# Every projection of a two-layer decoder trunk as one plain 32-bit product in place of three split ones, with a weight ring of seven places

## The reference

```
h += rms(mixer(rms(h)));  h += rms(swiglu(rms(h)));  h += (p @ W_ple) * sigmoid(h @ W_gate)
layer 0 mixer: gated DeltaNet
  qkv,z,beta,a = x @ gdn_w_in (1024 x 6176); qkv = silu(conv4(qkv)); q,k L2-normed
  chunked delta rule, 16 heads of 128;  out = (rms(o) * silu(z)) @ gdn_w_out (2048 x 1024)
after layer 0: kv = rms(h) @ kv_w (1024 x 1536), keys and values of three attention branches
layer 1 mixer: sparse attention, 16 heads of 64; q, gates = x @ nsa_w_qg (1024 x 1072); out = o @ nsa_w_o (1024 x 1024)
swiglu, both layers: (silu(x @ W_g) * (x @ W_u)) @ ffn_w_out, hidden 2816
ple, both layers: p @ ple_w_in (256 x 1024), h @ ple_w_gate (1024 x 1024)
```

## Time and profile before

| | |
|---|---|
| median of 3 runs | 969.92 us (969.77 to 970.20) |
| the profiled execution's own time | 970.94 us |
| its span, first to last instruction | 968.9 us |
| TensorE matmul busy | 925.4 us, 96% |
| TensorE weight load busy | 781.1 us, 81% |
| VectorE busy | 583.3 us, 60% |
| ScalarE busy | 519.7 us, 54% |
| moved by DMA | 138.30 MB, mean 143 GB/s |

### The profile page before, as it was taken

How to read it: one execution, slowest core, us unless ns; L and a number is a source line. 1 busy time by engine, 2 the same in 40 slices (tenths; PEclk the granted TensorE clock), 3 DMA queues, 4 the chain that set the end, 5 groups by cost and what they waited for, 6 DMA issues and landing times.

```text
span 968.9 us, 14299 instructions
## 1 busy us (share of the span) xinstructions
PE 925.4 (96%) x5437; PEld 781.1 (81%) x5437; DVE 583.3 (60%) x965; ACT 519.7 (54%) x919; POOL 23.3 (2%) x47
## 2 busy tenths in 40 slices
PE   5999989999999999999999999998889999999998
PEld 5989978797887877888887788997567788888776
DVE  5767775666566575555544666656857555554465
ACT  6554555766766446444443548245865644444352
POOL 5000000000000000000000000000000000000000
PEclk9999999999999999999999999999999999999999
DMA  9941202021112556777655654420024566565552
GB/s 320 330 138 44 88 0 88 10 78 44 45 45 90 193 166 212 236 232 240 192 175 171 208 186 154 150 88 2 1 89 141 169 191 193 174 191 176 171 187 100
DMA packets 105755, 138.30 MB, mean 143 GB/s; under 512 B 4569, under 2 KB 76514, under 8 KB 105698
## 3 DMA queue, kind: packets, MB, share of 16 engines
q1 hardware_dynamic: 103200, 130.04, 42.0%
q0 software_dynamic: 2160, 7.36, 2.1%
q10 hardware_dynamic: 338, 0.12, 0.0%
HBM read 136.45 MB, written 1.05 MB: 142 GB/s over the span
## 4 chain that ended last, share of the span: by engine, by line
PE 79%; ACT 10%; DVE 8%; issue 2%; ACTq 0%; DMA 0%; SPq 0%; DVEq 0%
PE ps L490 16%; PE ps L492 16%; PE ps L491 16%; PE ps L469 4%; PE ps L474 4%; PE ps L476 4%; PE ps L475 4%; DVE w_lo L1561 3%; ACT w_hi L1098 3%; PE ps L705 3%; PE ps L723 3%; PE ps L938 1%; PE ps L984 1%; ACT qkvT L1495 1%; PE ps L608 1%
## 5 line engine op out<-in xcount | busy, mean ns | idle before, releaser
L1561 DVE TENSOR_TENSOR w_lo<-w_raw,w_hi 128x2048 fp32r<-128x2048 f32 (+2 forms) x100 | 220.7, 2207 | 203.4 <-ACT w_hi L1098 203.3
L1098 ACT ACTIVATE w_hi<-w_raw 128x2048 fp32r<-128x2048 f32 (+2 forms) x100 | 184.4, 1844 | 191.0 <-PE ps L492 150.0
L490 PE MATMUL ps<-w_hi,x_hi 128*128 128x512 f32 x480 | 193.0, 402 | 7.4 <-DVE gdn L1772 2.2
L492 PE MATMUL ps<-w_hi,x_lo 128*128 128x512 f32 x480 | 187.7, 391 | 0.0
L491 PE MATMUL ps<-w_lo,x_hi 128*128 128x512 f32 x480 | 187.2, 390 | 0.0
L490 PEld LDWEIGHTS ps<-w_hi,x_hi 128*128 128x128 f32 x480 | 90.2, 188 | 29.7 <-issue 7.4
L492 PEld LDWEIGHTS ps<-w_hi,x_lo 128*128 128x128 f32 x480 | 90.1, 188 | 19.4
L491 PEld LDWEIGHTS ps<-w_lo,x_hi 128*128 128x128 f32 x480 | 90.3, 188 | 16.8
L474 PE MATMUL ps<-x_hi,w_hi 128*128 128x256 f32 x320 | 92.2, 288 | 0.3 <-DVE w_lo L1607 0.3
L475 PE MATMUL ps<-x_lo,w_hi 128*128 128x256 f32 x320 | 90.9, 284 | 0.0
L490 PE MATMUL ps<-w_hi,big 128*128 128x512 f32 x224 | 89.9, 401 | 1.0 <-DVE w_lo L1561 1.0
(11 more groups left out here) (309 smaller groups left out, 1492.0 us busy)
## 6 DMA issues: line engine op xcount, KB each, us to landing
w_raw<-in_ffn_w_in SPq DMA_DIRECT2D x88, 512.0 KB, 4.5
w_raw<-in_ffn_w_out SPq DMA_DIRECT2D x40, 512.0 KB, 4.1
w_raw<-in_gdn_w_in SPq DMA_DIRECT2D x28, 512.0 KB, 4.8
gdn<-in_gdn_w_in SPq DMA_DIRECT2D x20, 512.0 KB, 8.8
w_raw<-in_gdn_w_out SPq DMA_DIRECT2D x16, 512.0 KB, 4.5
w_raw<-in_ple_w_gate SPq DMA_DIRECT2D x16, 512.0 KB, 4.5
w_raw<-in_kv_w SPq DMA_DIRECT2D x12, 512.0 KB, 4.4
qkvT<-in_cmp_w POOLq DMA_DIRECT2D x8, 512.0 KB, 5.3
```

The costliest lines, as they stand in the source:

```text
L490: mm(o, hi, w_h, start=first and kk == 0, stop=False, skip_group_check=True)
L492: return mm(o, lo, w_h, start=False, stop=end and kk == n - 1, skip_group_check=True)
L1098: A(whi[:, place(stage, q), c0:c0 + n], ring_raw(u) if stage == "qkv" else raw[:, q, 0:n], ACT.Copy).then_inc(S["hi_done"], 1)
L1561: V.tensor_tensor(wlo[:, s, c0:c0 + n], ring_raw(u) if stage == "qkv" else raw[:, q, 0:n], whi[:, s, c0:c0 + n], ALU.subtract).then_inc(S[ ...
```

## The change

All fp32r tiles go, and with them every split of weights and activations. Each product is one plain float32 matmul, read from the raw weights where they landed. The raw weights get a ring of seven places through the whole kernel. SyncE loads unit u when TensorE has done unit u-7. A unit is one transfer of its whole size, save in fin and the first two of kv, which stay two transfers (their two column groups), and unit 0. TensorE waits for the transfer itself (`arrived`). The activation items, which both engines worked on in turn, are now made by ScalarE for even numbers and by VectorE for odd ones. The hardware loops of the fin stages are written out. The first items of the compression weights (`cmp_w1`) are loaded by GpSimd every four units of fin0 in place of every two. `big` and the attention outputs lie in other storage.

The diff, cut to its core:

```diff
+TRANSFERS = [2 if n.startswith("fin") or (n == "kv" and m < 2) else 1 for n, c in STAGES for m in range(2 * c)]
-RING = 6
+RING = 7
...
-        raw = sb("w_raw", [P, 2, 8 * UW])
-        whi = sb("w_hi", [P, 2, 8 * UW], F32R)
-        wlo = sb("w_lo", [P, 2, 8 * UW], F32R)
-        xhi = sb("x_hi", [P, KD, T], F32R)
-        xlo = sb("x_lo", [P, KD, T], F32R)
+        raw = sb("w_raw", [P, RING, 8 * UW])
+        xs = sb("x_normed", [P, KD, T])
...
+        def place(u):
+            return raw[:, u % RING, :]
+        def arrived(engine, u):
+            engine.wait_ge(ring[u % RING], sum(16 * TRANSFERS[v] for v in range(u % RING, u + 1, RING)))
+        def operand_ready(engine, n):
+            engine.wait_ge(S["x_dve" if n % 2 else "x_act"], n // 2 + 1)
...
+            for stage, n_pairs in STAGES:
+                for m in range(2 * n_pairs):
+                    u = U0[stage] + m
+                    if u == 0:
+                        continue
+                    if u >= RING:
+                        sp.wait_ge(S["unit_done"], u - RING + 1)
+                    load(stage, m)
...
-                pool.wait_ge(S["unit_done"], U0["fin0"] + 2 * part + 2)
+                pool.wait_ge(S["unit_done"], U0["fin0"] + 4 * part + 2)
...
-                mm(o, whi[:, q, col:col + P], xh(k), start=start, stop=False, skip_group_check=True)
-                mm(o, whi[:, q, col:col + P], xl(k), start=False, stop=False, skip_group_check=True)
-                return mm(o, wlo[:, q, col:col + P], xh(k), start=False, stop=stop, skip_group_check=True)
+                return mm(bank(b, 2, T)[:, tile, :], place(u)[:, col:col + P], x_(k), start=start, stop=stop,
+                          skip_group_check=True)
...
-                mm(o, hi, w_h, start=first and kk == 0, stop=False, skip_group_check=True)
-                mm(o, hi, w_l, start=False, stop=False, skip_group_check=True)
-                return mm(o, lo, w_h, start=False, stop=end and kk == n - 1, skip_group_check=True)
+                return mm(bank(b, NW), x_(k0 + kk, a), place(u)[:, kk * NW:(kk + 1) * NW], start=first and kk == 0,
+                          stop=end and kk == n - 1, skip_group_check=True)
...
-                pe.wait_ge(S["lo_done"], i * 2 + (U0[name] + q + 1))
+                arrived(pe, u)
...
-                with pe.Fori(1, 5) as i:
-                    block_(i * 2 + 1, 1, lambda: hidden_turned(i * 2, 0))
-                    block_(i * 2 + 2, 0, lambda: hidden_turned(i * 2 + 1, 1))
+                for i in range(1, 11):
+                    block_(i, i % 2, lambda: hidden_turned(i - 1, (i - 1) % 2))
...
             def x_item(n, dst, src, scale=None):
-                if n >= 2:
-                    act.wait_ge(S["xlo_done"], n - 1)
+                if n % 2:
+                    return
...
-            def x_item(n, dst, src, hi, scale=None):
-                dve.wait_ge(S["xhi_done"], n + 1)
+            def x_item(n, dst, src, scale=None):
+                if n % 2 == 0:
+                    return
```

More of the change, by code:

```diff
@@ L137, in build @@
         ost = sb("o_stats", [P, 3, TT, 4])
-        with nc.sbuf_tensor("big", [P, 2 * KF, T], F32R) as big:
-            pass
         gdn = sb("gdn", [P, 12800])
+        big = gdn[:, 0:KF * T].rearrange("p (k t) -> p k t", t=T)
         def views(base):
@@ L323, in _, with whole, pairs @@
         def _(sp):
-            def halves(q, dst, src, n):
+            def whole(u, dst, src, n):
+                sp.dma_start(dst[:, 0:n, :], src[:, 0:n, :]).then_inc(ring[u % RING], 16)
+            def pairs(u, src):
+                dst = place(u).rearrange("p (k s n) -> p k s n", s=2, n=UW)
                 for e in range(2):
-                    part = slice(0, n // 2) if e == 0 else slice(n // 2, n)
-                    sp.dma_start(dst[:, part, :], src[:, part, :]).then_inc(landed[q], 16)
@@ L330, in pairs @@
[L330 to L354, removed]
+                    sp.dma_start(dst[:, :, e, :], src[:, :, e, :]).then_inc(ring[u % RING], 16)
+            def load(stage, m):
+                u, n = U0[stage] + m, unit_width(stage, m)
+                narrow = place(u).rearrange("p (k n) -> p k n", n=UW)
+                wide = place(u)[:, 0:n].rearrange("p (k n) -> p k n", n=NW)
+                if stage in ("qkv", "q"):
+                    whole(u, narrow, source(stage, m // 2, m % 2), KD)
+                elif stage.startswith("fin"):
+                    i, q = divmod(m, 2)
+                    pairs(u, fin[int(stage[3])][:, 4 * q:4 * q + 4, :, i * UW:(i + 1) * UW])
+                elif stage == "kv" and m < 2:
+                    pairs(u, wvv[:, 4 * m:4 * m + 4, 1:3, UW:2 * UW])
+                elif stage == "kv":
+                    whole(u, narrow, kv_source(m), KD)
+                elif stage.startswith("pin"):
+                    whole(u, wide, pin[int(stage[3])][:, m, :].rearrange("p (c n) -> p c n", n=NW), 2)
+                else:
+                    whole(u, wide, wide_source(stage, m), n // NW)
@@ L356, in _ @@
             sp.dma_start(h[:, 0, :], x[0, 0:P, :]).then_inc(S["x_in"], 16)
             sp.dma_start(h[:, 1, :], x[0, P:T, :]).then_inc(S["x_in1"], 16)
-            first = raw[:, 0, :].rearrange("p (k n) -> p k n", n=UW)
+            first = place(0).rearrange("p (k n) -> p k n", n=UW)
             sp.dma_start(first[:, 0:4, :], source("qkv", 0, 0)[:, 0:4, :]).then_inc(S["w_first"], 16)
[L360 to L391, removed]
+            sp.dma_start(first[:, 4:8, :], source("qkv", 0, 0)[:, 4:8, :]).then_inc(ring[0], 16)
@@ L498, in unit_by_k, with unit_by_token @@
                     for a in range(TT):
-                        last = token_products(q, n, banks[a], xs, a, kk, k0, first, end)
+                        last = token_products(u, n, banks[a], x_, a, kk, k0, first, end)
                 last.then_inc(S["unit_done"], 1)
-            def unit_by_token(q, n, banks, xs, k0, first, end, first_done=None, ready=None, between=None):
+            def unit_by_token(u, n, banks, x_, k0, first, end, first_done=None, ready=None, between=None):
+                arrived(pe, u)
                 for a in range(TT):
@@ L1081, in table @@
                 n_tbl[0] += 1
-            def split(stage, q, i=0):
-                u = i * 2 + (U0[stage] + q)
-                n = unit_width(stage, i * 2 + q) if isinstance(i, int) else 4 * NW
-                if stage == "qkv":
-                    act.wait_ge(ring[u % RING], ring_count(u))
-                else:
-                    act.wait_ge(landed[q], i * 32 + (16 * U0[stage] + 16 + 16 * q - RING_OFF))
-                if stage.startswith("pin"):
-                    act.wait_ge(S["unit_done"], U0[stage] - 1)
-                elif stage.startswith("gate") and q == 0 and isinstance(i, int) and i == 0:
-                    act.wait_ge(S["unit_done"], U0[stage] - 2)
-                elif not isinstance(u, int) or u >= 2:
-                    act.wait_ge(S["unit_done"], u - 1)
-                c0 = DM * q if stage.startswith("pin") else 0
-                A(whi[:, place(stage, q), c0:c0 + n], ring_raw(u) if stage == "qkv" else raw[:, q, 0:n],
-                  ACT.Copy).then_inc(S["hi_done"], 1)
-            def split_halves(stage, q):
-                act.wait_ge(landed[q], 16 * U0[stage] + 16 + 16 * q - RING_OFF)
-                act.wait_ge(S["unit_done"], U0[stage] + q - 1)
-                for part, done in ((slice(0, 2 * NW), "hi_half"), (slice(2 * NW, 4 * NW), "hi_done")):
-                    A(whi[:, place(stage, q), part], raw[:, q, part], ACT.Copy).then_inc(S[done], 1)
             act.wait_ge(S["cst_dve"], 1)
@@ L1163, in post @@
                         extra(u)
-                if following.startswith("fin"):
-                    split_halves(following, 0)
-                else:
-                    split(following, 0)
-                    split(following, 1)
                 for a in range(TT):
@@ L1214, in _ @@
             for u in range(14):
-                split("qkv", u % 2, (u + 2) // 2)
                 taps(u)
@@ L1316, in delta @@
                     decay_a(j + 1, 1)
-                else:
-                    for part in range(4):
-                        quarter(U0["gout"], part)
                 o_out(1, j)
@@ L1401, in ffn_and_ple @@
                 block_(0, 0, False)
-                with act.Fori(0, 5) as i:
-                    block_(i * 2 + 1, 1, True)
-                    block_(i * 2 + 2, 0, True)
+                for i in range(1, 11):
+                    block_(i, i % 2, True)
                 def extra(u):
@@ L1700, in _ @@
             for u in range(15):
-                if u < 14:
-                    split("qkv", u % 2, (u + 2) // 2)
                 if u == 14:
@@ L1821, in delta @@
                 V.tensor_copy(vn[:, 1], bank(2, 4, P)).then_inc(S["vn_sb"], 1)
-                if j < 3:
-                    z_quarter(8 * j + 8)
-                else:
-                    for part in range(4):
```

(1 more changed line is left out.)

445 lines of the change are left out of this document (118 added, 327 removed).

## The result

The changed kernel took 1112.78 us, the median of four runs (1112.66 to 1112.78), beside 970.06 us for the kernel before in the same session. The ratio is 1.147, with a 95% interval of 1.145 to 1.149. The forecast was 1122, with a range of 1102 to 1146. The span grew from 968.9 to 1110.7 us, by 141.8.

The account below looks back on a forecast made before the run. TensorE's product rate was taken as the bound: plain products add 162.6 us and removed waits give back 10, so 969.92 + 152.6 = 1122.5, stated as 1122 us, with a range of 1102 to 1146.

Parts of the forecast that it names:

- What bounds the kernel: Whole kernel: TensorE's pace of taking products is the bound, its matmuls busy for 925.4 of 968.9 us.
- Price of a plain product: TensorE: a plain float32 product costs 0.855 us at 512 columns and 0.44 at 256, dearer than three fp32r matmuls.
- Sum of the products: All products on TensorE, wide and narrow: plain ones add 162.6 us, with none of it hidden.
- Waits given back: TensorE's waits, mainly for split results: removing the splits gives back 10 us, with ends of 3 and 27.8.
- The range: Kernel time from 1102 to 1146 us: cheap prices with 22 us gained, to dear prices with 16 us gained.
- full idle gain: Lower bound of the range: all inner idle time of TensorE returns, at most 27.8 us, entered there as 22.
- Costs put at nothing: TensorE's weight loads, weight transfers, GpSimd's compression weights and alternating x items: all covered, adding no time.
- Four passes at the price of fp32r ones: Plain products in a stream: four passes each at the split pace, adding 227.5 us, time 1187; chance 0.06.
- An uncovered weight load: After each of 1184 products on TensorE: 0.09 us of load not covered, 107 us, time 1229; chance 0.03.
- All inner idle time gone: TensorE's waits inside the kernel: all close without splits, -27.8 us in place of -10, time 1105; chance 0.07.
- The other side: Split chain on ScalarE and VectorE is the bound: 174 us go, 162.6 come, time 958, faster; chance 0.02.

Follow-up runs that it names:

- e1: Changed kernel with each plain product replaced by three fp32r matmuls on a fixed weight tile, no splits, ring of six: 951.22 us, 0.979 of the kernel before.
- e6: e1 with bf16 in place of fp32r for the fixed tile and activations, ring of five places: 905.51 us, 0.932 of the kernel before.
- e2: Changed kernel with every unit except the first loaded in two transfers of half its size: 1112.52 us.
- e3: Changed kernel with a ring of two places for raw weights in place of seven: 1120.65 us.
- e7: e1 with one fp32r matmul per product in place of three: 603.5 us.
- e4: Kernel before with its hi and lo split parts held as bf16 in place of fp32r, still three products: 940.53 us, ratio 0.967.
- e5: e4 with three places for the weights' hi and lo parts in place of two, fin loops written out: 932.44 us, 0.960 of the kernel before.

## Why the prediction was right, point by point

- **What bounds the kernel.** Right. TensorE's pace is the time: e1, e6 and the changed kernel share a frame but for the places of the ring (six, five and seven), no wait for a transfer of weights stands in their lists, and the differences between them came out as passes times spacing, to about 2 us.
- **Price of a plain product.** 0.855 us at 512 columns, measured 0.859; 0.44 at 256, measured 0.435. Two pairs of isolated products in the trace before, with the starts of their followers, gave it to half a per cent. The stretch, where the follower comes late, was no guide to a stream, and keeping it as an end only was right.
- **Sum of the products.** 162.6 us forecast, 161.6 by e1 against the changed kernel. Counting the 64 products of the delta rule in full was nearly right too: 64 x 0.176 = 11.3 us, and the stretch grew by 183.2 - 172.9 = 10.3.
- **Waits given back.** The step that failed in its size. This term was forecast at 10 us; the two spans, 968.9 and 949.4 of e1, give 19.5, which is nearly the whole of the 9 us by which the forecast was high. The forecast took the 7.6 us that the page lists for the earlier trace rows and added 2.4 for all else. Those 7.6 went as said, but they were not all. By distances of starts the waits for split results were 9.7 + 3.8 = 13.5 us: the list leaves out the quarters of the z stage (1.1 us) and has the first product of gout without a releaser (1.9), and most listed waits are 0.16 to 0.24 us shorter than the distance that they add. The modelled end of a record (0.39 us shown, 0.23 apart) covers the first part of a pause. Another 4.2 us were waits for other results of VectorE. By the records TensorE's idle time fell by only 12.9 us; most of the rest is this hidden part. It can be seen only as a distance of starts, as in the kernel before at the start of fin0, where each product should start 0.68 us after the one before it:

```profile
358.24 0.48 PE L490 MATMUL ps<-w_hi,x_hi 128*128 128x512 f32 x1
...
359.32 0.50 PE L490 MATMUL ps<-w_hi,x_hi 128*128 128x512 f32 x1
...
360.12 0.40 PE L490 MATMUL ps<-w_hi,x_hi 128*128 128x512 f32 x1
...
360.98 0.50 PE L490 MATMUL ps<-w_hi,x_hi 128*128 128x512 f32 x1
```

  From 358.24 to 360.98 there are three products in 2.74 us, 0.7 more than 3 x 0.683, while the timeline marks no idle time before any of them. The ends I gave, 3 and 27.8 us, held it. What no run tells apart is why the 4.2 us of other VectorE results came sooner: the splits that no longer stood before them in VectorE's order, or the rest of the new frame.
- **The two errors.** Products and waits missed in the same direction, by 1 and by 9.5 us, so no larger error hides behind the 0.8% that the time was off.
- **The range.** It was worked out with 22 and 16 us given back, and calls the 22 the full idle gain, which the text has as 27.8. With the term's own ends, 27.8 and 3, the sums give 1097 to 1159 us. The result lies inside both.
- **Costs put at nothing.** Weight loads: 0.19 us beside a pass of 0.43. Transfers: e2, no difference; e3, 8 us even with two places; e7, enough for a kernel of 600 us.
- **The rivals.** Four passes at the price of fp32r ones (1187) would need 0.46 us a record; it is 0.43. The Trainium skill's four passes ("FP8 and Floating Point Precision", "TensorE Precision Notes") agree with 0.859 / 4 = 0.215 us for 512 columns, which is the bf16 pass of e4, 0.216: a plain product costs four passes of the cheap kind and an fp32r one is a dearer kind. An uncovered weight load (1229) is not there. All inner idle time gone (1105) did not come: the waits for `qkvT` in the attention loop, 3.2 + 2.8 + 2.0 + 1.3 = 9.3 us in the list above, are what the earlier trace rows had before the change. The other side (958, the chain's 18% as lost time) is refuted by e1, which removes the whole chain of splits and gains 20 us of the 174.

## What to carry to other kernels

- Before replacing n cheap passes by one dear instruction, find one isolated instance of the dear form in the trace and take the distance from its start to its follower's: 3 x 0.228 against 0.859 decides here, and it was all in the trace before. Work taken off engines that are not the bound gives back only the waits for its results, most of them at stage starts, here 20 us for 550 us of removed busy time (311.5 + 238.3).
- The share of an engine in the chain of waits is not time to be gained; 18% stood there and 2% was real.
- Where a split is made anyway, choose the type by the pass: bf16 parts made the kernel 3% faster than fp32r ones at a lower precision. The faster TensorE then waits longer for the splits, and one more place between the splitting engines and itself, with the fin loops written out, made it 4%.
- Waits listed in a profile are a lower bound where the ends of records are modelled. Two traces with the same instructions in the same order give the whole cost, from start to start, and its places.

## What the runs showed of the hardware

- An fp32r matmul of 512 columns takes 0.228 or 0.234 us from start to start, by its operands, a bf16 one 0.216 and each record of a plain float32 one 0.43. At 256 columns it is 0.12, 0.11 and 0.217. The operand that matters is the stationary one: in e1 the moving tile is the same everywhere, and 216 matmuls on `big` take 50.69 us, 0.235 each, beside 0.228 on `x_normed`. In e6, with bf16, both take 0.216. What about `big` makes an fp32r matmul dearer, no run shows.
- A short pause can cost clock. In e4 TensorE had almost nothing to do from about 115.1 to 117.8 us, waiting for VectorE (2.4 us). The granted clock behind it (columns as in e3):

```profile
116.00:118.00 2.00, 0.23 (x1) 0.24 (x2) 2.00 (x5) 0.43 (x2) 0.00 (x0) 0.73 0.00 0
118.00:120.00 2.00, 2.00 (x10) 2.00 (x11) 2.00 (x6) 0.12 (x1) 0.00 (x0) 0.50 0.00 0
120.00:122.00 2.00, 2.00 (x12) 2.00 (x11) 1.35 (x4) 0.89 (x2) 0.00 (x0) 0.50 0.00 0
122.00:124.00 2.00, 2.00 (x8) 1.66 (x8) 0.71 (x3) 0.18 (x1) 0.00 (x0) 0.56 0.00 0
124.00:126.00 2.00, 2.00 (x9) 1.11 (x8) 1.11 (x3) 0.84 (x2) 0.00 (x0) 1.00 0.00 0
```

  TensorE worked at the 1.2 GHz level for over 5 us and lost half of that. In e3 a wait of 2.4 us for a transfer was followed by the same fall, and there it cost 1.7 us. The same wait as in e4 was 1.6 us in the kernel before, with a clock of 1.00 behind it, and 0.8 us in the profiled run of e5. In the changed kernel, whose waits are 1.1 us at most after the start, all 40 slices are at 9 tenths or more.
